# Feed-forward stage: order of additions, place of a block sum, and which engine makes the high parts

## The reference

```python
h = rms_norm(x, norm_ffn_pre[l])
u = causal_dwconv(h @ ffn_w_up[l], ffn_conv_w[l]) + ffn_conv_b[l]   # 1024 -> 2 x 2816, 3 taps over positions
gate, up = jnp.split(u, 2, axis=-1)
x = x + rms_norm((jax.nn.silu(gate) * up) @ ffn_w_down[l], norm_ffn_post[l])
```

## Time and profile before

| | |
|---|---|
| median of 3 runs | 2286.94 us |
| profiled execution, own time | 2289.83 us |
| its span on the core | 2287.8 us |
| PE busy | 2186.1 us (96%) |
| DVE busy | 1328.3 us (58%) |
| ACT busy | 823.2 us (36%) |
| POOL busy | 1148.3 us (50%) |
| feed-forward loop and tail | about 650 to 1262 us |

### The profile page before, as it was taken

How to read it: one execution, slowest core, us unless ns; L and a number is a source line. 1 busy time by engine, 2 the same in 40 slices (tenths; PEclk the granted TensorE clock), 3 DMA queues, 4 the chain that set the end, 5 groups by cost and what they waited for, 6 DMA issues and landing times.

```text
span 2287.8 us, 27893 instructions
## 1 busy us (share of the span) xinstructions
PE 2186.1 (96%) x9634; PEld 1684.8 (74%) x9634; DVE 1328.3 (58%) x1366; ACT 823.2 (36%) x1321; POOL 1148.3 (50%) x842
## 2 busy tenths in 40 slices
PE   7999999999899999999998989999999999999998
PEld 5777755577687777777786667777767777888787
DVE  6864356537786666555658887666665456411223
ACT  4343256533333333332332353555344334200112
POOL 3533410167657666666668753222345553444475
PEclk9999999999999999999999999999999999999999
DMA  5111100043211111111113330010001111111153
GB/s 201 56 37 37 37 10 10 10 147 113 99 56 42 51 55 55 55 46 48 46 43 108 111 134 29 28 32 33 28 29 46 46 37 37 48 54 46 46 166 120
DMA packets 38353, 139.02 MB, mean 61 GB/s; under 512 B 4356, under 2 KB 4740, under 8 KB 37516
## 3 DMA queue, kind: packets, MB, share of 16 engines
q1 hardware_dynamic: 30960, 111.39, 15.2%
q10 hardware_dynamic: 7324, 26.69, 3.2%
HBM read 121.24 MB, written 16.78 MB: 60 GB/s over the span
## 4 chain that ended last, share of the span: by engine, by line
PE 74%; DVE 8%; issue 6%; POOL 5%; ACT 4%; DMA 1%; SPq 0%; DVEq 0%; POOLq 0%; ACTq 0%
PE PG L850 8%; PE PG L856 8%; PE PG L855 8%; PE PG L1434 5%; PE PG L1440 5%; PE PG L1439 5%; PE PG L1205 2%; POOL WH L696 2%; DVE VU L3209 2%; POOL WL L699 2%; DMA WR<-weights 1%; PE PO L1505 1%; PE PO L1227 1%; PE PO L1339 1%; PE PO L1343 1%
## 5 line engine op out<-in xcount | busy, mean ns | idle before, releaser
L696 POOL TENSOR_TENSOR WH<-WR,zero 128x512 fp32r<-128x512 f32 x268 | 310.8, 1160 | 838.6 <-PE PG L850 360.9
L699 POOL TENSOR_TENSOR WL<-WR,WH 128x512 fp32r<-128x512 f32 x268 | 389.1, 1452 | 21.0
L709 POOL TENSOR_TENSOR WL<-WR,WH 128x512 fp32r<-128x512 f32 x169 | 272.3, 1620 | 181.5 <-ACT WH L2126 181.5
L1434 PE MATMUL PG<-HH,WH 128*128 128x512 f32 x544 | 226.1, 416 | 5.7 <-ACTq L2431 2.7
L850 PE MATMUL PG<-HH,WH 128*128 128x512 f32 x528 | 213.3, 404 | 2.2 <-POOL WL L699 1.5
L1440 PE MATMUL PG<-HH,WL 128*128 128x512 f32 x544 | 213.2, 392 | 0.0
L1439 PE MATMUL PG<-HL,WH 128*128 128x512 f32 x544 | 212.2, 390 | 0.0
L856 PE MATMUL PG<-HH,WL 128*128 128x512 f32 x528 | 206.5, 391 | 0.0
L855 PE MATMUL PG<-HL,WH 128*128 128x512 f32 x528 | 206.4, 391 | 0.0
L2126 ACT ACTIVATE WH<-WR 128x512 fp32r<-128x512 f32 x169 | 105.1, 628 | 264.7 <-POOL WR L723 82.0
L723 POOL TENSOR_TENSOR WR<-WR 128x512 f32<-128x512 f32 x76 | 116.7, 1535 | 23.2 <-DMA WR<-weights 14.5
(11 more groups left out here) (640 smaller groups left out, 5379.8 us busy)
## 6 DMA issues: line engine op xcount, KB each, us to landing
WR<-weights SPq DMA_DIRECT2D x196, 512.0 KB, 3.5
X<-x_spill ACTq DMA_DIRECT2D x16, 512.0 KB, 4.6
x_spill<-X ACTq DMA_DIRECT2D x6, 1024.0 KB, 4.7
RAW<-x SPq DMA_DIRECT2D x8, 512.0 KB, 7.7
x_spill<-X ACTq DMA_DIRECT2D x1, 4096.0 KB, 12.6
X<-x_spill ACTq DMA_DIRECT2D x1, 4096.0 KB, 12.2
y<-RAW SPq DMA_DIRECT2D x7, 512.0 KB, 5.0
x_spill<-X ACTq DMA_DIRECT2D x4, 512.0 KB, 3.5
```

Source lines behind the costliest of these rows:

```text
L696: pool.tensor_tensor(WH[:, slot, part], WR[:, slot, part], zero[:, :].to_broadcast([P, HALF]), ALU.add).then_inc(w_hi, 1)
L699: pool.tensor_tensor(WL[:, slot, part], WR[:, slot, part], WH[:, slot, part].bitcast(F32), ALU.subtract).then_inc(w_split, 1)
L709: pool.tensor_tensor(part_of(WL, k), raw, part_of(WH, k).bitcast(F32), ALU.subtract).then_inc(u_lo, 1)
L1434: m = pe.matmul(out, WH[:, slot, w], HH[:, b, cut], start=b == 0, stop=False)
```

## The change

1. **Order of the additions on DVE.** In a turn the second tile's `first_adds` come ahead of the first tile's `block_product`, which was ahead of them. In the tail `last.first_adds()` comes ahead of the product of the last turn's second tile in the same way.
2. **Place of the fourth sum.** `combine(4)` writes to `b.raw(6)`, now the half `lower_1`, so the slot with the two `upper` blocks is free once that sum is made. SP starts the load into slot 0 on `u_sum` (sum 4 made) and into slot 1 on `u_lo` (low part 6 made); slots are no longer swapped for the second tile.
3. **High parts of gated products on ACT.** `product_high` (ACT, `ACT.Copy`) takes the place of `split_high` (DVE `tensor_copy`), for all 22 tiles. ACT waits for `f_prod`, DVE's `split_low` waits for ACT's count `f_silu_hi`, which now counts SiLUs and high parts.
4. **High parts of the last weights on ACT.** For the first 8 half-units (4 units) of `last_downs` ACT makes the high part (`high_last`) and POOL the low part only (`low_last`).

```diff
-        RAW_PARTS = ((0, 0), (0, 0), (1, 0), (0, 0), (0, 1), (1, 1), (0, 1))
+        RAW_PARTS = ((0, 0), (0, 0), (1, 0), (0, 0), (0, 1), (1, 1), (1, 0))
...
-                return WR[:, (unit + self.second) % 2, halves(q)]
+                return WR[:, unit, halves(q)]
...
-                for n, (done, s) in enumerate(((2, 0), (4, 1), (10, 1), (11, 0), (17, 0), (18, 1))):
-                    sp.wait_ge(u_lo, PARTS * i + done)
-                    load_at(6 * i + (FFN_RAW + 2 + n), s)
+                for n, (semaphore, done) in enumerate((
+                        (u_lo, PARTS * i + 2), (u_lo, PARTS * i + 4),
+                        (u_sum, Blocks(i).summed(4)), (u_lo, Blocks(i).part(6)),
+                        (u_sum, Blocks(i, 1).summed(4)), (u_lo, Blocks(i, 1).part(6)))):
+                    sp.wait_ge(semaphore, done)
+                    load_at(6 * i + (FFN_RAW + 2 + n), n % 2)
...
-                combine(4, upper_2, upper_2, upper_1, ALU.subtract, 5)
+                combine(4, b.raw(6), upper_2, upper_1, ALU.subtract, 5)
...
+            def low_last(n):
+
+                slot, part = (n // 2) % 2, halves(n % 2)
+                pool.wait_ge(w_hi, 2 * FFN_RAW + n + 1)
+                pool.tensor_tensor(WL[:, slot, part], WR[:, slot, part], WH[:, slot, part].bitcast(F32),
+                                   ALU.subtract).then_inc(w_split, 1)
...
+            def product_high(product_done, x, hi=GH, cut=slice(0, S)):
+
+                act.wait_ge(f_prod, product_done)
+                act.activation(hi[:, x, cut], PRD[:, cut], ACT.Copy).then_inc(f_silu_hi, 1)
...
                 turn_highs(i)(3)
+                product_high(first.tile(0), 0)
                 first_copy(first)
...
                 for q in range(3):
                     act.wait_ge(u_done, second.product(4 + q))
                     high_down(q, i + 1)
+                    if q == 0:
+                        product_high(first.tile(1), 1)
...
+            act.wait_ge(u_done, tail.product(1))
+            product_high(tail.tile(0), 0, GH_LAST)
             second_copy(tail)
+            def high_last(n):
+
+                u, slot, part = n // 2, (n // 2) % 2, halves(n % 2)
...
+                act.activation(WH[:, slot, part], WR[:, slot, part], ACT.Copy).then_inc(w_hi, 1)
+
+            high_last(0)
             block_tap(tail, 1)
+            high_last(1)
             block_tap(tail, 0)
+            high_last(2)
+            high_last(3)
             block_silu(tail, 2)
+            high_last(4)
+            high_last(5)
+            for cut in (LEFT_HALF, RIGHT_HALF):
+                product_high(tail.tile(1), 1, GH_LAST, cut)
...
+            def split_low(high_done, x, hi=GH, lo=GL, cut=slice(0, S)):
+
+                dve.wait_ge(f_silu_hi, high_done)
+                dve.tensor_tensor(lo[:, x, cut], PRD[:, cut], hi[:, x, cut].bitcast(F32),
+                                  ALU.subtract).then_inc(f_lo, 1)
...
-                block_product(b)
-                split_high(b.tile(1), 1)
...
                 t.first_adds()
-                split_low(1).then_inc(f_lo, 1)
+                block_product(b)
+                split_low(b.twice_tile(2), 1)
                 t.fourth_add()
...
+            last.first_adds()
             block_product(t.b)
-            dve.wait_ge(u_done, tail.product(1))
-            split_high(t.b.tile(1), 0, GH_LAST)
-            last.first_adds()
-            split_low(0, GH_LAST, GL_LAST).then_inc(f_lo, 1)
+            split_low(t.b.twice_tile(2), 0, GH_LAST, GL_LAST)
```

More of the change, by code:

```diff
@@ L520, in program @@
         LAST_PT = KT // 2
+        LAST_HIGHS = KT
         def last_group(n):
@@ L663, in _ @@
             with sp.Fori(0, TURNS) as i:
-                for n, (done, s) in enumerate(((2, 0), (4, 1), (10, 1), (11, 0), (17, 0), (18, 1))):
-                    sp.wait_ge(u_lo, PARTS * i + done)
-                    load_at(6 * i + (FFN_RAW + 2 + n), s)
-            for s, done in ((0, 7), (1, 6)):
-                sp.wait_ge(u_lo, PARTS * TURNS + done)
-                load(wts[FFN_RAW + RAW_AHEAD + s], s)
+                for n, (semaphore, done) in enumerate((
[4 more added lines that the diff above has]
+                    load_at(6 * i + (FFN_RAW + 2 + n), n % 2)
+            tail = Blocks(0, tail=True)
+            sp.wait_ge(u_sum, tail.summed(4))
+            load(wts[FFN_RAW + RAW_AHEAD], 0)
+            sp.wait_ge(u_lo, tail.part(6))
+            load(wts[FFN_RAW + RAW_AHEAD + 1], 1)
             with sp.Fori(FFN_RAW // 2 + 1, UNITS // 2) as i:
@@ L784, in _ @@
             block_sums(tail)
[L785 to L790, removed]
+            for n in range(LAST_HIGHS):
+                low_last(n)
+            with pool.Fori(FFN_RAW // 2 + LAST_HIGHS // 4, AHEAD // 2 - 1) as i:
                 for n in range(2):
@@ L2121, in tile_silu @@
                     act.wait_ge(f_lo, tile_no)
-                act.activation(PRD[:, :], VG[:, :], ACT.Silu).then_inc(f_silu, 1)
+                act.activation(PRD[:, :], VG[:, :], ACT.Silu).then_inc(f_silu_hi, 1)
             def high(k, raw):
@@ L2231, in turn_body @@
                 second_copy(second)
-                return second
+                return first, second
             with act.Fori(0, TURNS - 1) as i:
-                second = turn_body(i)
+                first, second = turn_body(i)
                 for q in range(3):
@@ L2246, in _ @@
                 next_highs(2)
-            second = turn_body(TURNS - 1)
+            first, second = turn_body(TURNS - 1)
             tail = Blocks(0, tail=True)
@@ L2250, in _ @@
                 high_block(tail, k)
+                if k == 0:
+                    product_high(first.tile(1), 1)
             block_tap(second, 0)
@@ L3155, in tile @@
                 g.wait_free(dve, 1)
[L3156 to L3169, removed]
+                product(2 * tile_no + 1)
+            def split_low(high_done, x, hi=GH, lo=GL, cut=slice(0, S)):
+                dve.wait_ge(f_silu_hi, high_done)
+                dve.tensor_tensor(lo[:, x, cut], PRD[:, cut], hi[:, x, cut].bitcast(F32),
+                                  ALU.subtract).then_inc(f_lo, 1)
             def block_product(b):
                 primed(dve, f_taps, b.taps(2))
-                product(b.tile(1))
+                product(b.twice_tile(1))
             class Tile:
@@ L3289, in _ @@
             accumulated(banks)
-            split_product(3, 0)
-            with step.loop(0, TURNS - 1, 6) as i:
+            split_low(6, 0)
+            with step.loop(0, TURNS - 1, 4) as i:
                 t = turn_body(i)
@@ L3326, in _ @@
             block_product(tail)
[L3327 to L3330, removed]
+            for n, cut in enumerate((LEFT_HALF, RIGHT_HALF)):
+                split_low(tail.twice_tile(2 + n), 1, GH_LAST, GL_LAST, cut)
             def accumulate_half(n):
```

27 lines of the change are left out of this document (19 added, 8 removed).

## The result

The changed kernel takes 2263.3 us (median of 4 runs, 2261.02 to 2263.53), the kernel before 2287.35 us (4 runs, 2286.9 to 2287.86). The ratio is 0.9893 (95% interval 0.9875 to 0.991): 24.05 us off. The profiled execution of the changed kernel took 2263.22 us with a span of 2261.3; its span is 26.5 us shorter than that of before, whose own execution lay 2.9 us above the median then known.

The account below looks back on a forecast made before the run. The loop was taken as PE work plus one hole a turn, waiting for DVE's addition. Hole 17.0, clock 3.2 and tail 3.5 sum to 23.7 us off the 2286.94 median: 2263.2 us, range 2257 to 2277.

Parts of the forecast that it names:

- the hole: Loop, second tile's sixth product: PE starts 1.97 us late for DVE's addition; closing saves 2.13 us a turn, 17.0 in eight.
- the clock: Loop: with no hole, the granted clock's two falls of 1.62 us each should go, 3.2 us, bounds 0 and 3.2.
- POOL's low part beside PSUM-sourced additions: Loop, sixth product's operand: additions stay outside the SBUF lock, so it takes 1.3 us, done 0.4 us ahead of need.
- the forecast's other bound: POOL's low part for the sixth product at 2.27 us ends at 890.1 and leaves a hole of 0.5 us.
- The high part on ACT: Loop, ahead of PE's down projection: slower than on DVE by 0.4 us, hidden by a margin of 0.5 us.
- Rivals A and B: A: new small wait in the loop, 2275, chance 0.17. B: ACT's high part late on weight load, 2297, chance 0.05.
- The tail: Up to PE's wait for the sum: 1.3 + 0.2 + 1.6 = 3.1 us earlier, taken as 3.5, bounds 0 and 6.
- this rule: DVE and POOL instructions reading two SBUF tiles run one behind the other; their shared port is a lock, the loser blocks.
- Rival C: Loop holes close but time is paid back by another clock fall or slower tail: 11 us off, 2276, chance 0.08.
- Rival D: Loop: the order does not act, additions still come at 890.8; 2286 us, chance 0.04.

Follow-up runs that it names:

- The order alone: Kernel before, only the second tile's three additions moved ahead of the first tile's product in a loop turn: 2268.31 us, ratio 0.9899.
- order undone: Changed kernel with DVE's product ahead of the second tile's additions again, high parts still on ACT, loads still early: 2269.36 us, ratio 0.9902.
- loads late: Changed kernel with sum 4 written where it was and loads started as before; order and ACT's high parts as changed: 2273.15 us, ratio 0.9922.
- high part later: Changed kernel with ACT's high part of the product behind the second high part of the down weights, not the first: 2270.57 us, ratio 0.9913.
- the earlier tap: Changed kernel with ACT's product high part ahead of weights' high parts, tail's first ACT tap one part earlier, DVE's zeroing behind the product: 2263.51 us, ratio 0.9879.

## Why the prediction was right, and where not

- **The bound and the hole: right.** Eight turns lost 20.1 us; forecast 17.0 for the hole and 3.2 for the clock. A turn takes 59.86 us over the eight; forecast 59.84. The order alone does this; the prediction had not said that the loop needs nothing else of the change.
- **POOL's low part beside PSUM-sourced additions: right.** 1.27 us, done 0.5 us ahead of PE; forecast 1.3 and 0.4. With the product ahead again it was late by 0.4; the forecast's other bound was 0.5.
- **The high part on ACT: hidden, by less than said.** The load took 3.67 us to ACT's start and DVE's low part 1.47 in place of 1.22; the margin was 0.27 us, forecast 0.5. Rivals A and B were that close: 0.63 us of ACT's work, or the late load, bring them on, at 7 to 10 us for the kernel. The prediction also says that rows agree with the 0.59 us that it works out for DVE's copy; its row has 0.70, and these runs 0.69. It made no term of the sum of it.
- **The clock: as forecast, on thinner ground.** None of the profiles with the hole closed shows a fall in the loop, and neither do three with holes of 0.4 to 1.0 us in every turn (order undone, loads late, high part later). So the two falls were seen only with the hole of 1.8 us, but another execution of before may have another number of them; its times spread by 7 us in one group of runs. There is one profile of before, so this stays open.
- **The tail: right in sign, mis-sized.** This is the term that was wrong: 3.5 us forecast, 7.4 measured. By its own parts: an earlier start of the last tile, by order and load, and the additions' order in the tail, 1.3 and 0.2 forecast, 1.1 together by the steps above (the loads undone by themselves cost 1.3); product's high parts 1.6, 2.8 measured; last weights' high parts on ACT next to nothing, as holes of PE, 2.65 measured; and 0.8 where both are undone. The step that failed was to price POOL's eight high parts by what PE waits for them. They act on DVE, which led to the sum: with them on POOL the last two taps take 4.26 us in place of 3.50 and the product 2.15 in place of 1.23. The prediction had used this rule for the loop and not for the tail.
- **The hit to 0.1 us is luck.** The forecast for the span was 2264.1 us and it measured 2261.3: the tail gave 3.9 us more than forecast, 1.6 were given back behind it, and 0.6 came ahead of the loop's first hole, where nothing was forecast. The forecast for the median, 2263.2, took the same 23.7 us off a median that lay some 2.5 us below the profiled execution of before. The span fell by 26.5 us and the median by 24.05; so the undersized tail and a slow execution of before cancelled. The 20 us of the loop are not luck: they were forecast from the hole and the clock's falls, and the traces show both gone.
- **Rival C** (paid back) happened for 1.6 us of 28.1, in that execution; the second one of the changed kernel took 1022.5 us behind the sum, less than before's 1023.5. **Rival D** is excluded by the empty list of waits.

## What to carry to other kernels

When one engine's queue holds a short instruction that PE waits for behind long ones that it doesn't, move the short one first; by itself that took 22.0 us off the median, with no work taken off any engine. Price an instruction that is moved off POOL or DVE not only by who waits for it but by what it stood in front of on the other of the two: here the instructions with two inputs from SBUF. A move of work to an engine that waits for a load needs the load earlier, and is worth nothing if the engine that it left was waiting there anyway.

## What was not expected of the hardware

- DVE's copy of a whole 128x1024 tile took 0.69 us where POOL was waiting and 1.66 us beside its subtractions; half a tile took 1.40 to 1.54 there. DVE's product, with two inputs from SBUF, went from 1.23 to 2.15 us with one POOL instruction in front of it. Additions of 128x512 with one input from PSUM took 0.67 to 0.69 us in every case, from the loop to the sum.
- Who is issued first decides here: the same sum on POOL took 1.30 us when issued ahead of a DVE tap and 2.15 behind it, and by this the earlier tap delayed PE by 0.85 us.
- Two profiled executions of one kernel agree to 0.2 us over the 65 us up to the sum and differ by 2.7 us behind it, where the granted clock of 16 us windows falls to 0.71 to 0.97 at 1280 to 1328 and 1376 to 1392 us in the one, and to 0.79 to 0.89 at 1264 to 1280 and 1296 to 1312 us in the other. Where it falls there is a matter of the execution.
